# Earlier norm statistics in a Conformer and latent-attention trunk on one core, and a residual loaded row by row

## The chip, the cores and the metric

One core of a Trainium2 chip runs the whole kernel. The metric is the device time of one launch in microseconds (us). The engines are TensorE (PE, matrix products), VectorE (DVE), ScalarE (ACT), GpSimd (POOL) and SyncE (SP, which here issues the DMAs). They run side by side, each in the order of its own program, and wait for one another by semaphores.

## The reference, cut to what matters

The program is two layers on a sequence of 512 rows of 1024 channels in float32. The change touches only the first, the convolution branch:

```
proj = h @ w_in + b_in                      # 1024 -> 3 * 2048
val, glu_gate, z = split(proj, 3)
u = val * sigmoid(glu_gate)
u = causal depthwise convolution of u, 31 taps, + conv_b
u = silu(layer_norm(u, norm_g, norm_b))     # over the 2048 channels
u = u * silu(z)
y = u @ w_out + b_out                       # 2048 -> 1024
h = layer_norm(alpha * h + y, ln_g[0], ln_b[0])
```

The second layer (a shared latent key and value, 16 attention heads, a gate, an output projection, a norm) reads this h. Products are made to float32 accuracy from split operands: each factor is cut into a rounded high part and a low rest, and three matrix products (low by high, high by low, high by high) are summed.

## The kernel before, in words

**Layout.** The 2048 channels of the branch are 16 tiles of 128 partitions by 512 rows of sequence (CT = 16). The input projection makes 48 such tiles ("chunks"): for each tile first value and gate, then 16 chunks for z. A chunk is 24 matmuls (8 slices of the contraction, 3 products each; `columns`, L1445, with the matmuls in L1421). Then the output projection takes its weights in 16 chunks too, 24 matmuls each: chunks 0 to 7 for the left half of the 1024 outputs, 8 to 15 for the right half; chunk n multiplies the branch tiles 2(n mod 8) and 2(n mod 8) + 1 by four blocks of rows. They are called output chunks here, and the z chunks are numbered 0 to 15.

**Weights.** SP loads a chunk into one of two raw buffers. ACT writes its high part (L719) into one of four slots, POOL the low part (L561); PE then waits for both. A raw buffer is free once POOL has taken the low part, so that a load (L402, L437) follows POOL; a slot is free once PE has used it, so that ACT's high part of chunk c waits for PE to finish chunk c - 4. ACT empties PE's bank of z chunk i through silu into `z_a` (`keep_z`, L808), and PE takes four banks in turn for the z chunks.

**The norm over channels.** DVE makes 12 of the 16 convolutions, tap after tap, and adds all tiles into `csum` (L1090). PE multiplies that by a matrix of ones (L1493, "mean") ahead of z chunk 11 (MEAN_AT). DVE then subtracts the mean from each of the 16 tiles (L1158, `centered`), ACT squares each (L819, L823) into four buffers, DVE sums the even squares (L1164, between its subtractions) and POOL the odd ones (L616). Ahead of z chunk 14 (VAR_AT) PE sums both over the channels with matmuls one column wide (L1500, "variance"); it waits there for both sums. DVE adds the epsilon (L1183), POOL raises to -1/2 (L638), ACT makes four diagonal blocks (L865), and ahead of z chunk 15 (SPREAD_AT) PE spreads the factor over all partitions (L1486, "spread"). SQUARES says behind which z chunk ACT squares which tiles and POOL adds the odd ones: tiles 0 to 3 with chunk 14's weights, 4 to 8 with chunk 15's, 9 to 15 with the first output chunk's.

**The branch.** With the spread factor there, each tile t goes through DVE (times the factor, L1188), ACT (silu, L829), DVE (times `z_a`, L1195), ACT (high part, L835) and DVE (low part, L1199), in three rotating banks. ACT's program runs 17 steps of this loop in one piece, with the rest of its work put in by hand at t = 3 (keep z chunk 15) and t = 9 (the high part of output chunk 3). Only behind the loop does it split the weights of output chunk 4 and later. PE's output chunk n needs the tiles it multiplies.

**The residual.** After the last z chunk, SP loads the input rows again (`res`, 2 MB, L445) and three broadcast rows of the norm and of the bias (L446 to L448), all on one semaphore. Only behind them come the loads of output chunks 4 to 15. ACT scales the four rows of `res` by alpha (L883) behind its splits 5 to 8, POOL adds the bias to them (L656) behind its splits 6 to 9. DVE waits for all four rows before it adds the first product to them (L1220).

Of the kernel before, what the change touches and what calls it, by code (L numbers as in the profile page):

```python
# [32 lines left out]
P = 128  # L33
BANK = 512
DEPTH = 2
D_MODEL = 1024
# [19 lines left out]
CT = CONV_WIDTH // P  # L56
RT = SEQ // P
# [12 lines left out]
Z0 = 2 * CT  # L70
OUT0 = Z0 + CT
# [6 lines left out]
SLOTS = 4  # L78
# [34 lines left out]
def trunk_kernel(nc, x, positions, ln_g, ln_b, a_w_in, a_b_in, a_conv_w, a_conv_b, a_norm_g,  # L113
# [3 lines left out]
    x_rows = x.rearrange("b (r p) d -> p (b r) d", p=P)  # L117
# [10 lines left out]
    with ExitStack() as ctx:  # L128
        def sem(name):
            return ctx.enter_context(nc.semaphore(name))  # L130
# [10 lines left out]
        def at(name, base, offset_words, shape, dtype=F32):  # L141
            return nc.alloc_sbuf_tensor_at(name, shape, dtype, offset=base + 4 * offset_words)
# [75 lines left out]
        res = at("res", reg_xt, 0, [P, RT, D_MODEL])  # L218
        ln_rows = at("ln_rows", reg_xt, 8 * TILE, [P, 3, D_MODEL])
# [52 lines left out]
        def piece(parts, lo, hi):  # L272
# [39 lines left out]
            sem("var_ready"), sem("rstd_cols_ready"), sem("rstd_diag_ready"), sem("rstd_spread"), sem("stat_step"))  # L312
        scaled, silu_done, gated, g_hi_ready, g_lo_ready = (
            sem("scaled"), sem("silu_done"), sem("gated"), sem("g_hi_ready"), sem("g_lo_ready"))
        res_landed, res_scaled, res_ready = sem("res_landed"), sem("res_scaled"), sem("res_ready")
        y_done, y_step, var_row_ready, rstd_row_ready, rstd_step, row_ready = (
            sem("y_done"), sem("y_step"), sem("var_row_ready"), sem("rstd_row_ready"),
            sem("rstd_step"), sem("row_ready"))
# [30 lines left out]
        def added_before(n):  # L349

            return sum(1 for _, k in shared_taps[:n] if k > 0)

        SHARES_BEGIN = SHARED_TILES[0] + 2
        MEAN_AT, VAR_AT, SPREAD_AT = 11, 14, 15
        SQUARES = {14: range(0, 4), 15: range(4, 9), OUT0 - Z0: range(9, CT)}
        GATE_BANK = (4, 5, 6)
        RSTD_BANK = 7
        VSUM_BANK = 6
# [36 lines left out]
        def _(sp):  # L395
            def raw_free(c):

                wait(sp, w_hi_ready, c - RAW_SLOTS + 1)
                wait(sp, w_lo_ready, c - RAW_SLOTS + 1)
# [33 lines left out]
            def load_output(c0, n, source):  # L433

                raw_free(c0 + n)
                half, k = n // PASS, 2 * (n % PASS)
                sp.dma_start(w_raw[(c0 + n) % 2][:].rearrange("p (k m) -> p k m", k=2),  # L437
                             source[k:k + 2, :, half * BANK:(half + 1) * BANK].rearrange("k p m -> p k m")
                             ).then_inc(w_landed[(c0 + n) % 2], 16)
# [2 lines left out]
                load_output(OUT0, n, w_out_a)  # L442

            sp.wait_ge(w_used, OUT0)
            sp.dma_start(res[:], x_rows).then_inc(res_landed, 16)  # L445
            sp.dma_start(ln_rows[:, 0, :], ln_g[0:1, :].broadcast_to([P, D_MODEL])).then_inc(res_landed, 16)  # L446
            sp.dma_start(ln_rows[:, 1, :], ln_b[0:1, :].broadcast_to([P, D_MODEL])).then_inc(res_landed, 16)
            sp.dma_start(ln_rows[:, 2, :], a_b_out.broadcast_to([P, D_MODEL])).then_inc(res_landed, 16)  # L448
            for n in range(SLOTS, CT):
                load_output(OUT0, n, w_out_a)  # L450
            for n in range(LATENTS):
                c = LAT0 + n
                raw_free(c)
                if n < KV:
                    load_columns(c % 2, w_down, n * P)
                elif n == KV:
                    halves = w_raw[c % 2][:].rearrange("p (k b m) -> p b k m", b=2, m=ROPE)
                    for b in range(2):
                        sp.dma_start(halves[:, b], w_down[:, :, KV_RANK:KV_RANK + ROPE]
                                     ).then_inc(w_landed[c % 2], 16)  # L460
                else:
                    load_columns(c % 2, w_in_b, (n - KV - 1) * P)
# [80 lines left out]
        def _(pool):  # L543
# [74 lines left out]
            def add_odd_squares(tiles):  # L618
                for t in tiles:
                    if t % 2 == 1 and t > 1:  # L620
                        add_odd_square(t)

            for i in range(CT):
# [7 lines left out]
                for n in z_taps(i):  # L631
                    add_product(n)
                add_odd_squares(SQUARES.get(i, ()))
            split_lo(OUT0, OUT0 % 2, OUT0 % SLOTS)
            add_odd_squares(SQUARES[CT])

            pool.wait_ge(var_ready, 1)
            nc.gpsimd.tensor_tensor(rstd_cols[:], var_cols[:], minus_half[:], ALU.pow).then_inc(rstd_cols_ready, 1)  # L638
# [10 lines left out]
            for k in range(CT):  # L649
                c = OUT0 + k  # L650
                if k > 0:
                    split_lo(c, c % 2, c % SLOTS)
                if 6 <= k < 6 + RT:
                    r = k - 6
                    pool.wait_ge(res_scaled, r + 1)
                    nc.gpsimd.tensor_tensor(res[:, r, :], res[:, r, :], ln_rows[:, 2, :], ALU.add  # L656
                                            ).then_inc(res_ready, 1)
# [57 lines left out]
        def _(act):  # L715
# [54 lines left out]
            def keep_conv(m):  # L770
                t = MATRIX_TILES[m]
                act.wait_ge(*((diag_used, len(TAP_GROUPS)), (pe_conv_done, 1))[m])
                nc.scalar.activation(acc[:, t, :], bank[MATRIX_BANK[m]][:], ACT.Identity,
                                     bias=vec[:, V_CONVB + t:V_CONVB + t + 1]).then_inc(pe_conv_kept, 1)


            for q in range(2 * RT):
                r, half = q // 2, q % 2
# [26 lines left out]
            def keep_z(i):  # L805

                act.wait_ge(w_used, Z0 + i + 1)
                nc.scalar.activation(z_a[:, i, :], bank[i % 4][:], ACT.Silu,  # L808
                                     bias=vec[:, V_BIN + 2 * CT + i:V_BIN + 2 * CT + i + 1]
                                     ).then_inc(evacuated, 1)  # L810
# [5 lines left out]
            def square(t):  # L816
                act.wait_ge(centered, t + 1)
                if t < 2:
                    nc.scalar.activation((bank[VSUM_BANK], vsum_odd)[t][:], acc[:, t, :], ACT.Square  # L819
                                         ).then_inc((vsum_done, vsum_odd_done)[t], 1)  # L820
                else:
                    wait(act, (vsum_done, vsum_odd_done)[t % 2], t // 2 - 1)
                    nc.scalar.activation(sq[t % 4][:], acc[:, t, :], ACT.Square  # L823
                                         ).then_inc((squared_even, squared_odd)[t % 2], 1)
# [12 lines left out]
            def output_split(k):  # L837
                c = OUT0 + k
                split_hi(c, c % 2, c % SLOTS, landed_value(c))

            for i in range(CT):
                z_split(i)
                if i == 0:
                    keep_value_gate(CT - 1, (CT - 1) % ROUND)
                    for g in range(len(TAP_GROUPS)):
                        conv_matrices(1, g)
                        for n in matrix_taps(g):
                            tap_times_u(n)
                    keep_conv(0)
                if i == 2:  # L850
                    keep_conv(1)
                for t in SQUARES.get(i, ()):
                    square(t)
                if i >= 3:
                    keep_z(i - 3)
                for n in z_taps(i):
                    tap_times_u(n)
            output_split(0)
            for t in SQUARES[CT]:
                square(t)  # L860
            keep_z(CT - 3)
            output_split(1)
            act.wait_ge(rstd_cols_ready, 1)
            for b in range(RT):
                nc.scalar.activation(rstd_diag[:, b * P:(b + 1) * P], ident[:], ACT.Copy,  # L865
                                     scale=rstd_cols[:, b:b + 1]).then_inc(rstd_diag_ready, 1)
            keep_z(CT - 2)
            output_split(2)
            for t in range(CT + 1):
                if t == 3:  # L870
                    keep_z(CT - 1)
                if t == 9:
                    output_split(3)
                if t < CT:
                    branch_silu(t)
                if t >= 1:
                    branch_hi(t - 1)
            for k in range(SLOTS, CT):
                output_split(k)
                if 5 <= k < 5 + RT:  # L880
                    r = k - 5
                    act.wait_ge(res_landed, 64)
                    nc.scalar.activation(res[:, r, :], res[:, r, :], ACT.Copy, scale=ALPHA  # L883
                                         ).then_inc(res_scaled, 1)

# [2 lines left out]
            for q in range(2 * RT):  # L888
                r, half = q // 2, q % 2
# [149 lines left out]
        def _(dve):  # L1039
            for q in range(2 * RT):  # L1040
                r, half = q // 2, q % 2
# [205 lines left out]
                                                   ).then_inc(row_ready, 1)  # L1247

            dve.wait_ge(res_ready, RT)
            def turned_lo(r):  # L1250
                for q in (2 * r, 2 * r + 1):
                    cut = (slice(None), slice(4 * (q % 2), 4 * (q % 2) + 4), slice(r * P, (r + 1) * P))
                    dve.wait_ge(ht_hi_ready, q + 1)
                    nc.vector.tensor_tensor(ht_lo[cut], bank[q][:].rearrange("p (k n) -> p k n", k=4),  # L1254
                                            ht_hi[cut].bitcast(F32), ALU.subtract).then_inc(ht_lo_ready, 1)
# [504 lines left out]
```

## Time and profile before

| what | value |
|---|---|
| median of 3 timed runs | 899.72 us (899.52 to 900.37) |
| the profiled execution's own time | 898.75 us |
| its span | 897.0 us |
| PE busy | 860.2 us, 96% of the span |
| DVE busy | 607.1 us, 68% |
| POOL busy | 486.4 us, 54% |
| ACT busy | 399.5 us, 45% |
| mean granted clock of PE | 0.982 |

The table is the first part of the profile's page. The span runs from the first to the last instruction of one profiled execution, and 1.75 us of the execution's own time lie outside it. Times of rows below count from the start of the span. The granted clock is TensorE's: 1.00 is 2.4 GHz and 0.50 is 1.2 GHz.

### The profile page before, as it was taken

What the parts mean: (1) busy time and instruction counts of PE and PEld (TensorE: products, weight loads), DVE (VectorE), ACT (ScalarE), POOL (GpSimd) and SP (SyncE); (2) the same over time, 40 slices, a digit from 0 to 9 for tenths busy, and PEclk for the clock granted to TensorE, in tenths of its full rate; (3) what the DMA queues carried; (4) which work ended last, traced back from release to release, by engine and by line L of the source; (5) the groups of instructions that cost most, each with busy time, mean ns of one, the idle gap of its engine ahead of it and who ended that gap; (6) DMA issues with size and microseconds to landing.
All of it is one profiled execution on the core that took longest, in us unless ns stands there. A gap on an engine that the chain in (4) does not pass through costs nothing.

```text
span 897.0 us, 11802 instructions
## 1 busy us (share of the span) xinstructions
PE 860.2 (96%) x4059; PEld 714.5 (80%) x4059; DVE 607.1 (68%) x1077; ACT 399.5 (45%) x694; POOL 486.4 (54%) x272
## 2 busy tenths in 40 slices
PE   5999999999999989799899999999999999989996
PEld 4888888888888767588698788878988888978885
DVE  2899999999999538420842292039778779768207
ACT  3655444436653447621332344146555565545110
POOL 3578888877995462384654437424324424126443
PEclk7999999999999979899999999999999999999999
DMA  6242333320044325243043334321232320223212
GB/s 205 77 119 76 104 96 95 95 75 0 1 118 118 94 71 188 73 134 98 1 139 109 95 93 130 80 68 41 61 82 70 82 80 13 71 94 141 94 48 95
DMA packets 111351, 78.99 MB, mean 88 GB/s; under 512 B 14023, under 2 KB 98093, under 8 KB 111277
## 3 DMA queue, kind: packets, MB, share of 16 engines
q1 hardware_dynamic: 111308, 78.44, 29.1%
q8 instruction: 24, 0.39, 0.2%
q14 instruction: 19, 0.16, 0.1%
HBM read 71.87 MB, written 2.10 MB: 82 GB/s over the span
## 4 chain that ended last, share of the span: by engine, by line
PE 88%; DVE 4%; issue 2%; POOL 2%; ACT 1%; DMA 1%; SPq 0%; POOLq 0%; DVEq 0%; ACTq 0%
PE bank L1421 83%; PE bank L1686 2%; DMA x_in<-in_x_dram 1%; PE bank L1675 1%; PE bank L1676 1%; DVE bank L1195 1%; DVE g_lo L1199 1%; POOL vsum_odd L616 1%; POOL w_lo L561 1%; DVE res L1245 0%; ACT w_hi L719 0%; PE bank L1432 0%; PE bank L1500 0%; DVE pt_lo L1360 0%; DVE fg_lo L1405 0%
## 5 line engine op out<-in xcount | busy, mean ns | idle before, releaser
L561 POOL TENSOR_TENSOR w_lo<-w_raw,w_hi 128x1024 fp32r<-128x1024 f32 x103 | 253.7, 2472 | 205.6 <-ACT w_hi L719 179.8
L1105 DVE SCALAR_TENSOR_TENSOR bank<-u,conv_w,bank 128x512 f32<-128x512 f32 x348 | 233.5, 750 | 0.9
L1421 PE MATMUL bank<-xt_hi,w_lo 128*128 128x512 f32 x384 | 154.6, 403 | 1.4 <-DVE xt_lo L1044 1.4
L719 ACT ACTIVATE w_hi<-w_raw 128x1024 fp32r<-128x1024 f32 x103 | 107.0, 1053 | 104.8 <-PE bank L1421 52.0
L1421 PE MATMUL bank<-xt_lo,w_hi 128*128 128x512 f32 x384 | 153.4, 399 | 0.0
L1421 PE MATMUL bank<-xt_hi,w_hi 128*128 128x512 f32 x384 | 153.1, 399 | 0.0
L1421 PEld LDWEIGHTS bank<-xt_hi,w_lo 128*128 128x128 f32 x384 | 73.7, 192 | 19.4 <-DVE xt_lo L1044 1.8
L1421 PEld LDWEIGHTS bank<-xt_lo,w_hi 128*128 128x128 f32 x384 | 73.5, 191 | 17.5 <-issue 0.5
L1421 PEld LDWEIGHTS bank<-xt_hi,w_hi 128*128 128x128 f32 x384 | 73.5, 191 | 17.4
L588 POOL TENSOR_TENSOR acc<-acc,tap_product 128x512 f32<-128x512 f32 x60 | 77.9, 1298 | 8.5 <-ACT tap_product L753 1.6
L669 POOL TENSOR_TENSOR bundle_lo<-bundle_raw,bundle_hi 128x1024 fp32r<-128x1024 f32 (+1 forms) x16 | 47.1, 2961 | 62.3 <-ACT bundle_hi L917 62.3
L1421 PE MATMUL bank<-ht_hi,w_lo 128*128 128x512 f32 (+2 forms) x200 | 76.5, 383 | 2.5 <-DVE ht_lo L1254 2.5
L1421 PE MATMUL bank<-ht_lo,w_hi 128*128 128x512 f32 (+2 forms) x200 | 75.7, 379 | 0.0
L1421 PE MATMUL bank<-ht_hi,w_hi 128*128 128x512 f32 (+2 forms) x200 | 75.7, 379 | 0.0
L1220 DVE SCALAR_TENSOR_TENSOR res<-res,bank 128x512 f32<-128x512 f32 x16 | 10.9, 681 | 91.7 <-PE bank L1421 65.3
L1421 PE MATMUL bank<-w_hi,g_lo 128*128 128x512 f32 x128 | 51.8, 405 | 6.1 <-issue 6.1
L753 ACT ACTIVATE tap_product<-u,conv_w 128x512 f32<-128x512 f32 x60 | 41.7, 718 | 32.3 <-POOL acc L588 32.0
L982 ACT ACTIVATE prob<-prob,neg_top 128x512 f32<-128x512 f32 (+1 forms) x64 | 35.5, 555 | 43.5 <-DVE neg_top L1319 43.5
L1421 PE MATMUL bank<-w_hi,fg_lo 128*128 128x512 f32 x128 | 50.9, 398 | 1.2 <-DVE fg_lo L1405 1.2
L1421 PE MATMUL bank<-w_hi,g_hi 128*128 128x512 f32 x128 | 51.0, 399 | 0.0
L1421 PE MATMUL bank<-w_lo,g_hi 128*128 128x512 f32 x128 | 51.0, 398 | 0.0
L1421 PE MATMUL bank<-w_hi,fg_hi 128*128 128x512 f32 x128 | 50.6, 395 | 0.0
(198 smaller groups left out, 1815.4 us busy)
## 6 DMA issues: line engine op xcount, KB each, us to landing
w_raw<-in_a_w_in_dram SPq DMA_DIRECT2D x48, 512.0 KB, 3.7
w_raw<-in_b_w_in_dram SPq DMA_DIRECT2D x20, 512.0 KB, 3.6
w_raw<-in_a_w_out_dram SPq DMA_DIRECT2D x16, 512.0 KB, 3.7
w_raw<-in_b_w_out_dram SPq DMA_DIRECT2D x16, 512.0 KB, 3.5
bundle_raw<-in_b_w_uq_dram SPq DMA_DIRECT2D x16, 256.0 KB, 3.8
x_in<-in_x_dram SPq DMA_DIRECT2D x4, 512.0 KB, 7.0
res<-in_x_dram SPq DMA_DIRECT2D x1, 2048.0 KB, 7.8
bundle_raw<-in_kv_w_uk_dram SPq DMA_DIRECT2D x8, 256.0 KB, 3.0
```

The costliest lines, as they stand in the source:

```text
L561: nc.gpsimd.tensor_tensor(w_lo[slot][:], w_raw[raw][:], w_hi[slot][:].bitcast(F32), ALU.subtract).then_inc(w_lo_ready, 1)
L588: nc.gpsimd.tensor_tensor(acc[:, t, :], acc[:, t, :], tap_product[n % 2][:], ALU.add).then_inc(product_added, 1)
L616: nc.gpsimd.tensor_tensor(vsum_odd[:], vsum_odd[:], sq[t % 4][:], ALU.add).then_inc(vsum_odd_done, 1)
L669: nc.gpsimd.tensor_tensor(bundle_lo[slot][part][:], bundle_raw[:, lo:hi], bundle_hi[slot][part][:].bitcast(F32), ALU.subtract).then_inc(bu ...
L719: nc.scalar.activation(w_hi[slot][:], w_raw[raw][:], ACT.Copy).then_inc(w_hi_ready, 1)
L753: nc.scalar.activation(tap_product[n % 2][:], u[:, t, k:k + SEQ], ACT.Copy, scale=tap).then_inc(product_ready, 1)
L982: nc.scalar.activation(block_, block_, ACT.Exp, bias=neg_top[:, b:b + 1], scale=SM_SCALE, accum_out=denom[:, b:b + 1]).then_inc(exp_done, 1)
L1105: nc.vector.scalar_tensor_tensor(out=bank[CONV_BANK[slot]][:] if k < TAPS - 1 else acc[:, t, :], in0=u[:, t, k:k + SEQ], scalar=conv_w[:, ...
L1195: nc.vector.tensor_tensor(inner[:], inner[:], z_a[:, t, :], ALU.mult).then_inc(gated, 1)
L1220: nc.vector.scalar_tensor_tensor(out=rows_half, in0=rows_half, scalar=scale, in1=bank[RT * half + r][:], op0=ALU.mult, op1=ALU.add).then_i ...
L1421: last = nc.tensor.matmul(out_ap, a, b, start=(start and n == 0 and m == 0), stop=(stop and n == len(parts) - 1 and m == 2))
L1686: last = nc.tensor.transpose(bank[to_bank][:, first + k * P:first + (k + 1) * P], prob[:, (prob_at[b] + k) * P:(prob_at[b] + k + 1) * P], ...
```

## The change

Three things are changed together. The mean, variance and spread stand ahead of z chunks 10, 13 and 14 (before: 11, 14, 15). The squares follow: tiles 0 to 7 with chunk 13's weights, 8 to 15 with chunk 14's, none behind the output weights; ACT keeps each z chunk one step later, and the loop over the branch tiles has its inserted work at t = 3, 6 and 9. The residual and the broadcast rows are loaded in seven pieces, each behind the load of one output chunk, with semaphores of their own; ACT and POOL take the rows one step later.

```diff
-        res_landed, res_scaled, res_ready = sem("res_landed"), sem("res_scaled"), sem("res_ready")
+        res_landed = [sem(f"res_landed{r}") for r in range(RT)]
+        bias_landed, ln_a_landed = sem("bias_landed"), sem("ln_a_landed")
+        res_scaled, res_ready = sem("res_scaled"), sem("res_ready")
...
-        MEAN_AT, VAR_AT, SPREAD_AT = 11, 14, 15
-        SQUARES = {14: range(0, 4), 15: range(4, 9), OUT0 - Z0: range(9, CT)}
+        MEAN_AT, VAR_AT, SPREAD_AT = 10, 13, 14
+        SQUARES = {13: range(0, 8), 14: range(8, CT)}
...
             sp.wait_ge(w_used, OUT0)
-            sp.dma_start(res[:], x_rows).then_inc(res_landed, 16)
-            sp.dma_start(ln_rows[:, 0, :], ln_g[0:1, :].broadcast_to([P, D_MODEL])).then_inc(res_landed, 16)
-            sp.dma_start(ln_rows[:, 1, :], ln_b[0:1, :].broadcast_to([P, D_MODEL])).then_inc(res_landed, 16)
-            sp.dma_start(ln_rows[:, 2, :], a_b_out.broadcast_to([P, D_MODEL])).then_inc(res_landed, 16)
             for n in range(SLOTS, CT):
                 load_output(OUT0, n, w_out_a)
+                r = n - SLOTS - 1
+                if n == SLOTS:
+                    sp.dma_start(ln_rows[:, 2, :], a_b_out.broadcast_to([P, D_MODEL])).then_inc(bias_landed, 16)
+                elif r < RT:
+                    sp.dma_start(res[:, r, :], x_rows[:, r, :]).then_inc(res_landed[r], 16)
+                elif r == RT:
+                    sp.dma_start(ln_rows[:, 0, :], ln_g[0:1, :].broadcast_to([P, D_MODEL])).then_inc(ln_a_landed, 16)
+                elif r == RT + 1:
+                    sp.dma_start(ln_rows[:, 1, :], ln_b[0:1, :].broadcast_to([P, D_MODEL])).then_inc(ln_a_landed, 16)
...
             split_lo(OUT0, OUT0 % 2, OUT0 % SLOTS)
-            add_odd_squares(SQUARES[CT])
...
-                if 6 <= k < 6 + RT:
-                    r = k - 6
+                if 7 <= k < 7 + RT:
+                    r = k - 7
+                    if r == 0:
+                        pool.wait_ge(bias_landed, 16)
                     pool.wait_ge(res_scaled, r + 1)
...
+                if i >= 4:
+                    keep_z(i - 4)
                 for t in SQUARES.get(i, ()):
                     square(t)
-                if i >= 3:
-                    keep_z(i - 3)
...
             output_split(0)
-            for t in SQUARES[CT]:
-                square(t)
-            keep_z(CT - 3)
-            output_split(1)
+            keep_z(CT - 4)
             act.wait_ge(rstd_cols_ready, 1)
...
-            keep_z(CT - 2)
-            output_split(2)
+            output_split(1)
+            keep_z(CT - 3)
             for t in range(CT + 1):
                 if t == 3:
+                    output_split(2)
+                    keep_z(CT - 2)
+                if t == 6:
                     keep_z(CT - 1)
...
-                if 5 <= k < 5 + RT:
-                    r = k - 5
-                    act.wait_ge(res_landed, 64)
+                if 6 <= k < 6 + RT:
+                    r = k - 6
+                    act.wait_ge(res_landed[r], 16)
...
             dve.wait_ge(res_ready, RT)
+            dve.wait_ge(ln_a_landed, 32)
```

## Rows read from the trace of the kernel before

**Rows 1.** The page: busy time by engine; the chain that ended last, by engine.
```profile
PE 860.2 (96%) x4059; PEld 714.5 (80%) x4059; DVE 607.1 (68%) x1077; ACT 399.5 (45%) x694; POOL 486.4 (54%) x272
...
PE 88%; DVE 4%; issue 2%; POOL 2%; ACT 1%; DMA 1%; SPq 0%; POOLq 0%; DVEq 0%; ACTq 0%
```
**Rows 2.** Windows: stretch, its length, busy by engine, granted clock, DMA share, GB/s.
```profile
322.00:325.30 3.30, 0.00 (x0) 0.03 (x1) 0.69 (x1) 2.32 (x4) 2.87 (x3) 0.90 0.22 86
325.30:328.85 3.55, 3.54 (x17) 3.55 (x17) 0.00 (x0) 0.00 (x0) 0.00 (x0) 0.50 0.02 5
```
**Rows 3.** Timeline of PE: start, length, line, count, idle time before and its releaser.
```profile
303.30 1.02 PE L1493 MATMUL bank<-csum,ones 128*128 128x512 f32 x2
...
325.31 0.56 PE L1500 MATMUL bank<-ones,vsum 128*128 128x1 f32 x2 [4.19 <-POOL vsum_odd L616]
...
372.34 0.76 PE L1421 MATMUL bank<-w_hi,g_lo 128*128 128x512 f32 x1 [6.12 <-issue]
...
375.88 0.40 PE L1421 MATMUL bank<-w_hi,g_hi 128*128 128x512 f32 x1
...
447.59 0.66 PE L1421 MATMUL bank<-ht_hi,w_lo 128*128 128x384 f32 x1 [2.45 <-DVE ht_lo L1254]
```
**Rows 4.** The chain that ended last: start, length, what, with counts.
```profile
328.85 8.51 PE bank L1421 x24
337.36 0.86 PE bank L1486 x2
338.22 5.61 PE bank L1421 x24
...
632.61 1.09 PE bank L1686 x10
```
**Rows 5.** Timeline of DVE: the last sum, the subtractions, the branch's start and its pause.
```profile
296.75 0.69 DVE L1090 TENSOR_TENSOR csum<-bank,acc 128x512 f32<-128x512 f32 x1
304.35 3.08 DVE L1158 SCALAR_TENSOR_TENSOR acc<-bank,acc 128x512 f32<-128x512 f32 x5 [6.91 <-PE bank L1493]
...
338.26 1.29 DVE L1188 TENSOR_TENSOR bank<-acc,bank 128x512 f32<-128x512 f32 x2 [9.21 <-PE bank L1486]
...
345.22 0.70 DVE L1195 TENSOR_TENSOR bank<-bank,z_a 128x512 f32<-128x512 f32 x1 [0.31 <-ACT bank L829]
```
**Rows 6.** Timeline of ACT: an ordinary step, squares, diagonal blocks, tile 3, the loop's end.
```profile
297.92 0.69 ACT L808 ACTIVATE z_a<-bank,vec 128x512 f32<-128x512 f32 x1 [3.95 <-PE bank L1421]
298.51 1.05 ACT L719 ACTIVATE w_hi<-w_raw 128x1024 fp32r<-128x1024 f32 x1
...
317.08 2.18 ACT L823 ACTIVATE sq<-acc 128x512 f32<-128x512 f32 x4
...
330.20 1.28 ACT L865 ACTIVATE rstd_diag<-ident,rstd_cols 128x128 f32<-128x128 f32 x4 [5.62 <-POOL rstd_cols L638]
...
344.44 0.74 ACT L829 ACTIVATE bank<-bank,vec 128x512 f32<-128x512 f32 x1
...
368.77 1.99 ACT L719 ACTIVATE w_hi<-w_raw 128x1024 fp32r<-128x1024 f32 x2
```
**Rows 7.** Timeline of POOL: the odd squares, the power, two low parts.
```profile
319.63 5.53 POOL L616 TENSOR_TENSOR vsum_odd<-vsum_odd,sq 128x512 f32<-128x512 f32 x4
329.13 1.04 POOL L638 TENSOR_TENSOR rstd_cols<-var_cols,minus_half 128x4 f32<-128x4 f32 x1 [3.97 <-DVE var_cols L1183]
330.14 2.38 POOL L561 TENSOR_TENSOR w_lo<-w_raw,w_hi 128x1024 fp32r<-128x1024 f32 x1
```
**Rows 8.** Windows behind and around other gaps of PE, columns as in rows 2.
```profile
448.00:449.00 1.00, 1.00 (x4) 1.00 (x4) 1.00 (x2) 0.00 (x0) 0.92 (x2) 0.50 0.24 57
...
590.00:594.00 4.00, 2.49 (x11) 1.76 (x10) 0.69 (x1) 3.23 (x4) 1.57 (x1) 1.00 0.00 0
```
**Rows 9.** DMA issues from 300 to 430 us: count, KB each, us to landing.
```profile
w_raw<-in_a_w_out_dram SPq DMA_DIRECT2D x16, 512.0 KB, 3.7
res<-in_x_dram SPq DMA_DIRECT2D x1, 2048.0 KB, 7.8
```

## The prediction

> **What bounds the kernel now.** I read the page first. PE is busy for 96% of the span and makes 88% of the chain that ended last [rows 1], so only time in which PE stands still, or runs at half clock, can be won. Next the windows by granted clock around the norm: the clock is at 0.50 (1.2 GHz) over the whole variance step [rows 2]. Third, the timeline of PE. It stands still twice near the change: 4.19 us ahead of the variance matmuls, released by POOL's last odd square, and 6.12 us ahead of output chunk 4 [rows 3]. That second gap bears the name "issue", but the chain and ACT's timeline show who it is: ACT's high part of chunk 4 starts only at 368.77, at the end of the branch loop [rows 6]. Fourth, the lengths of chunks in the chain: z chunk 14 takes 8.51 us and z chunk 15 takes 5.61 [rows 4]. Last, the timelines of DVE, ACT and POOL, for the lengths of their steps.
>
> What these stalls cost, as a ceiling: 4.19 + 6.12 us of standing still; 8.51 - 5.61 = 2.9 us of half clock in chunk 14; the variance step, 3.54 us of chain between 325.31 and 328.85 [rows 2, 3]; and the first eight matmuls of output chunk 4, 375.88 - 372.34 = 3.54 us where eight take 5.58 x 8/24 = 1.86, so 1.7 us.
>
> **The unit steps.** A full-clock chunk is 5.58 us of PE: 5.61 in the chain with its tail [rows 4], and I take 5.58 since the last matmul of z chunk 9 releases ACT at 297.92 [rows 6] and the mean starts behind z chunk 10 at 303.30 [rows 3]; so z chunk 10 starts at 303.30 - 5.58 = 297.72. Mean and spread take 0.86 us of PE each (two matmuls) [rows 4]. DVE: five subtractions in 3.08 us [rows 5], so one per (3.08 - 0.69)/4 = 0.60. ACT: four squares in 2.18 [rows 6], 0.52 each, or DVE's pace where it waits for it. POOL: four odd squares in 5.53 [rows 7], about 1.4 each. A low part 2.4 [rows 7], a high part 1.0 [rows 6], the power 1.04 [rows 7], the four diagonal blocks 1.28 [rows 6].
>
> The variance step at full clock is not in this trace. Bounds: its 16 matmuls are load-bound and took 3.54 at half clock; ten transposes with loads of the same size took 1.09 us at full clock [rows 4], so 16 would take 1.74. I take 1.8, nearest to that row and half of 3.54, and keep 3.54 as the other end.
>
> **Mean at chunk 10.** It wants `csum`. DVE writes it at 296.75 + 0.69 = 297.44 [rows 5]; PE arrives at 297.72. So the mean fits with 0.3 us to spare, and what it costs is its place only. Nothing ahead of it moves on DVE. ACT's `keep_z` a step later costs nothing: ACT waited 3.95 us in such a step [rows 6], and PE needs that bank only four chunks on.
>
> **The sums.** Subtractions start 1.05 us behind the mean's start (304.35 - 303.30 [rows 3, 5]), at 298.8. DVE has 16 subtractions and 7 even sums, 23 x 0.60 = 13.8 us. Before, this run was cut in pieces: ACT came back to squares only behind weights and `keep_z`, which wait for PE. Now ACT does high part 13 (297.9 to 298.9), keeps z 9, and squares tiles 0 to 7 at DVE's pace, until 305.5. Then high part 14, z 10 (307.1), tiles 8 to 15; DVE loses 0.6 us there (its even sum 10 waits for square 8) and subtracts tile 15 by 312.6; ACT's square 15 is done at 313.3. POOL does low part 13, odd tiles 3, 5, 7 (306.9), low part 14 (309.3), then tiles 9, 11, 13 and 15 chained: 309.3 + 5.5 = 314.8. PE reaches the variance at 297.72 + 0.86 + 3 x 5.58 = 315.3. So the 4.19 us of standing still go, with 0.5 us to spare, and with them the cause of the half clock; the variance ends at 315.3 + 1.8 = 317.1.
>
> **The spread at chunk 14.** It wants the diagonal blocks at 317.1 + 5.58 = 322.7. Queued on POOL ahead of the power now: low part 15 (314.8 to 317.1) and the first output low part, whose high part ACT can make only when PE is through with z chunk 12 at 315.3 (316.4 done). So POOL: 317.1 to 319.5, power to 320.6; ACT's blocks to 321.9. 0.8 us to spare. Before, the blocks were there at 330.20 + 1.28 = 331.5 for a spread at 337.3 [rows 4, 6], some 6 us of room; most of that is used up.
>
> **The branch.** Spread starts at 322.7, so DVE scales tile 0 at 323.7 (before: 338.26 [rows 5]), 14.5 us earlier. ACT is ready: it makes output chunk 1's high part at 322.8 and keeps z 13, until 324.4, when tile 0 is scaled. One new wait stands in ACT's loop: at t = 3 it makes chunk 2's high part and keeps z 14, and both want z chunk 14, which ends at 322.7 + 0.86 + 5.58 = 329.1. Silu of tile 3 then starts at 329.2 + 1.0 + 0.6 = 330.8, or 7.0 us behind the first scale, where before it started 344.44 - 338.26 = 6.2 behind it [rows 5, 6] and stopped DVE for 0.31. Behind it silus 4 and on queue; DVE's next product comes 0.8 us late, and the whole loop with it. At t = 6 z 15 is kept at about 334.9 to 335.6; z chunk 15 ends at 334.7 and PE writes that bank again at 336.8: hidden. Output chunk 4 followed the first scale by 372.34 - 338.26 = 34.1 us [rows 3, 5]; now 34.1 + 0.8, so it starts at 358.6.
>
> **PE itself** gets to output chunk 4 at 329.1 + 5 x 5.58 = 357.0 (z 15, output 0 to 3; their tiles of the branch come at one per 1.92 us, twice per chunk, and are ready). So 1.6 us of standing still remain, set by the branch loop. I assume that this gap leaves the clock alone.
>
> **The residual.** Before: 2 MB and three rows of 0.5 MB in one piece ahead of output load 4. Now each piece follows a load that must wait for POOL's low parts: bias behind load 4 at 334.7; row 0 behind load 5 at about 344; row 1 behind load 6 at about 359; rows 2 and 3 one chunk apart. A load of 0.5 MB took 3.7 us and the 2 MB 7.8 [rows 9], and a chunk takes 5.58, so each row is there when ACT's split of the same step is: row r is issued ahead of weight load r + 6, and ACT asks for it behind split r + 6. POOL adds 2.4 us to its 2.4 for four steps, 4.8 of 5.58. The fourth row is ready a chunk later, near the end of output chunk 7, and DVE's half rows (about 5.5 us) lie beside chunk 8; the first row norm comes with chunk 12. I cost all this at nothing; without that cover a late row costs one for one.
>
> The Trainium skill speaks against the cut: "DMA: Bandwidth & Descriptors", section Bandwidth, asks for transfers of 1 MiB or more for at least 75% of peak. By that rule four rows take longer than one block, and the trace agrees: 4 x 3.7 = 14.8 us against 7.8 [rows 9]. It would change the time only in the slower rival below.
>
> **The sum.** Output chunk 4 starts 372.34 - 358.6 = 13.7 us earlier and runs at full clock (1.7): 15.4 us. Beside the ceiling: 4.2 + 2.9 + 1.7 (variance) + 6.1 + 1.7 = 16.6, less 1.6 left; the two agree within 0.4. All behind output chunk 4 moves along, since PE bounds it. From the execution profiled, 898.75 becomes 883.4; that execution is 1.0 us below the median of 899.72. On the median: 884.4.
>
> **Rivals.**
> *The clock still falls at the variance.* For: one-column matmuls and transposes are little work; behind some transposes and 2.45 us of standing still the clock was at 0.50 [rows 3, 8]. Against: a stretch with only 2.49 of 4.00 us of matmuls kept 1.00 [rows 8], and here 1.8 us of variance lie between full chunks. Cost: the variance at up to 3.54 instead of 1.8, and up to 2.9 us in chunk 13, 1.7 to 4.6 in all: near 887.
> The Trainium skill, "TensorE: Matmul & The Clock Gate", section on what is happening in Part 1, says that the throttled state is the default and activity releases it. By that rule the variance step is at risk although PE is never idle; the time would be this rival's.
> *A link is late.* The margins are 0.3, 0.5 and 0.8 us, out of chains of up to 17 us; 3% more on POOL's or ACT's chain and PE waits at variance or spread. It costs the lateness, 1 to 3 us, and with a fallen clock more: 886 to 889.
> *The clock falls in the gap ahead of output chunk 4*, 1.6 us of it: 1.7 us more, 886.1.
> *The gain is hidden* (within 0.2%): the mean would have to wait for `csum` by some 14 us. DVE's rows speak against it [rows 5].
> *Slower: the rows of the residual starve PE.* POOL and ACT take them in order, and a row that lands late holds back the next low part. It decides once a row and a weight load together take more than a chunk with 2 us of slack, 7.6 us; two loads at 3.7 are 7.4 if they do not overlap at all. With four rows landing late by up to 3.7 us and 1.7 us of clock each, 4 x 5.4 = 21.6 - 15.4 = 6.2 us slower, 905.9. Against it: loads before overlapped (the 2 MB in 7.8).
>
> **How the numbers follow.** Forecast 55%; fallen clock at the variance 17%; late link 14%; clock at chunk 4 6%; hidden 3%; slower 3%; 2% for more gain than the sum (no gap, cheaper variance: 882.7). The range, 882.8 to 889.2, holds all but some 15%. What a measurement of this kernel can tell from no change is about 0.2%, 1.8 us. Faster by more than that: 0.94; within it 0.03; slower 0.03.
>
> **What would show it.** Right: mean at 297.7 and variance at 315.3 with no idle time ahead of them; granted clock 1.00 and a chunk 13 of 5.6 us; spread at 322.7; a pause of DVE of some 1.1 us at the branch's tile 3; output chunk 4 at 358.6 behind 1.6 us of idle PE. Wrong: a window at 0.50 behind the variance (the clock rival); PE released by POOL's L616 or ACT's L865 (a late link); ACT's L719 or L883 waiting for DMA between chunks 5 and 11 with PE idle (the slower rival).

## The result, and the profile after

| | median us | runs | span of the profiled execution |
|---|---|---|---|
| before | 899.62 | 4 | 897.0 |
| changed | 886.88 | 3 | 884.3 |

The changed kernel took 886.41, 886.88 and 888.78 us; a fourth execution, 1065.4 us at a mean granted clock of 0.749, is left out, and with it the median of all four is 887.83. The ratio to the kernel before is 0.986 (95% interval 0.9836 to 0.9883): faster by 1.4%. The forecast was 884.4 in a range of 882.8 to 889.2. Run again on another chip, with experiments 6 to 8, the changed kernel took 885.68 us against 900.12 (ratio 0.9842, 0.9829 to 0.9856).

The page of the changed kernel, busy time and the chain by engine, as [rows 1]: PE is busy for 2.5 us less in a span 12.7 us shorter, so most of what went was time in which PE stood still. Its share of the chain is 92% instead of 88.

```profile
PE 857.7 (97%) x4059; PEld 712.7 (81%) x4059; DVE 606.3 (69%) x1077; ACT 399.4 (45%) x694; POOL 487.1 (55%) x272
...
PE 92%; DVE 2%; DMA 2%; SPq 1%; issue 1%; ACT 1%; POOL 0%; POOLq 0%; DVEq 0%; ACTq 0%
```

The chain that ended last, from z chunk 8 to the output projection (start, length, what):

```profile
289.85 9.30 PE bank L1430 x40
299.14 0.86 PE bank L1502 x2
300.00 16.73 PE bank L1430 x72
316.73 1.68 PE bank L1509 x16
318.41 5.68 PE bank L1430 x24
324.09 0.86 PE bank L1495 x2
324.94 33.59 PE bank L1430 x144
358.53 1.55 issue
360.09 61.83 PE bank L1430 x264
```

Before, pieces of POOL, ACT and DVE stood between PE's. Two of them, POOL's sum of odd squares ahead of the variance and DVE's low part in the branch loop:

```profile
319.68 1.25 POOL vsum_odd L616
...
345.92 0.60 DVE g_lo L1199
```

Now it is PE from end to end: mean, three chunks (16.73 = 3 x 5.58), variance in 1.68 us, chunk 13 in 5.68 (before, chunk 14 behind the variance took 8.51 [rows 4]), spread, six chunks, one gap of 1.55, and on. The clock, in windows with the columns of [rows 2], stays at full speed through the variance and through the gap:

```profile
316.00:318.00 2.00, 2.00 (x18) 1.86 (x16) 0.00 (x0) 1.17 (x2) 2.00 (x2) 1.00 0.04 8
318.00:320.00 2.00, 2.00 (x12) 1.69 (x12) 0.16 (x1) 0.46 (x1) 2.00 (x2) 1.00 0.07 17
...
358.00:360.00 2.00, 0.53 (x3) 0.09 (x1) 0.00 (x0) 0.49 (x1) 2.00 (x2) 1.00 0.00 0
360.00:362.00 2.00, 1.91 (x8) 1.61 (x9) 0.00 (x0) 0.00 (x0) 2.00 (x1) 1.00 0.31 92
```

The three engines that feed PE, by their timelines: DVE's last sum, its subtractions, its first product of the branch and its pause at tile 3 (as [rows 5]); ACT's last square, the diagonal blocks, silu of tile 3 and the end of its loop (as [rows 6]); POOL's last odd squares, the two low parts ahead of the power, and the power (as [rows 7]).

```profile
296.46 0.69 DVE L1098 TENSOR_TENSOR csum<-bank,acc 128x512 f32<-128x512 f32 x1
300.04 3.08 DVE L1166 SCALAR_TENSOR_TENSOR acc<-bank,acc 128x512 f32<-128x512 f32 x5 [2.89 <-PE bank L1502]
...
324.98 1.29 DVE L1196 TENSOR_TENSOR bank<-acc,bank 128x512 f32<-128x512 f32 x2 [6.37 <-PE bank L1495]
...
332.94 0.70 DVE L1203 TENSOR_TENSOR bank<-bank,z_a 128x512 f32<-128x512 f32 x1 [1.31 <-ACT bank L837]
```
```profile
313.76 0.63 ACT L831 ACTIVATE sq<-acc 128x512 f32<-128x512 f32 x1 [0.56 <-DVE acc L1166]
...
321.80 1.28 ACT L870 ACTIVATE rstd_diag<-ident,rstd_cols 128x128 f32<-128x128 f32 x4 [3.34 <-POOL rstd_cols L644]
...
330.64 1.06 ACT L727 ACTIVATE w_hi<-w_raw 128x1024 fp32r<-128x1024 f32 x1 [1.54 <-PE bank L1430]
...
332.17 0.74 ACT L837 ACTIVATE bank<-bank,vec 128x512 f32<-128x512 f32 x1
...
356.50 2.00 ACT L727 ACTIVATE w_hi<-w_raw 128x1024 fp32r<-128x1024 f32 x2
```
```profile
310.48 5.62 POOL L623 TENSOR_TENSOR vsum_odd<-vsum_odd,sq 128x512 f32<-128x512 f32 x4
316.06 4.71 POOL L568 TENSOR_TENSOR w_lo<-w_raw,w_hi 128x1024 fp32r<-128x1024 f32 x2
320.73 1.04 POOL L644 TENSOR_TENSOR rstd_cols<-var_cols,minus_half 128x4 f32<-128x4 f32 x1
```

Compare their ends with PE's starts, which are those of its timeline: odd squares ready at 310.48 + 5.62 = 316.1, variance at 316.57; blocks ready at 321.80 + 1.28 = 323.1, spread at 323.93. Both fit, by 0.5 and 0.8 us.

### The profile page after: what moved, and what is told of

It is laid out like the page before. It is cut to its first block, busy times and chain, and to the rows that moved or that the text cites. A ratio compares the mean times of both kernels' runs of the same rounds, so it can differ in the third digit from the quotient of the medians.

```text
span 884.3 us, 11806 instructions
## 1 busy us (share of the span) xinstructions
PE 857.7 (97%) x4059; PEld 712.7 (81%) x4059; DVE 606.3 (69%) x1077; ACT 399.4 (45%) x694; POOL 487.1 (55%) x272
## 4 chain that ended last, share of the span: by engine, by line
PE 92%; DVE 2%; DMA 2%; SPq 1%; issue 1%; ACT 1%; POOL 0%; POOLq 0%; DVEq 0%; ACTq 0%
PE bank L1430 88%; PE bank L1695 1%; DMA pos_int<-in_positions_dram 1%; PE bank L1684 1%; PE bank L1685 1%; SPq L421 1%; DVE pt_lo L1369 0%; DVE res L1253 0%; DVE prob L1339 0%; DMA qr_stack<-qr_lo 0%; SPq L414 0%; ACT prob L990 0%; PE bank L1568 0%; PE bank L1622 0%; PE bank L1509 0%
## 5 line engine op out<-in xcount | busy, mean ns | idle before, releaser
L699 POOL TENSOR_TENSOR qr_raw<-qr_raw,cos 128x512 f32<-128x512 f32 x8 | 10.4, 1294 | 72.6 <-DMA qr_swap<-qr_raw 72.6
```

The costliest lines, as they stand in the source:

```text
L699: nc.gpsimd.tensor_tensor(qr_raw[:], qr_raw[:], cos[:], ALU.mult).then_inc(rope_step, 1)
```

## The experiments

The start of the span takes longer in one profile than in another, by up to 3.6 us. PE begins z chunk 10, or the mean that stands ahead of it, at 297.7 us before the change, at 299.0 in the changed kernel and at up to 301.3 in the experiments. The difference is there by 36 us of the span, and the clock has a part in it. PE between 24 and 30 us, before and changed, with the columns of [rows 2]:

```profile
24.00:30.00 6.00, 6.00 (x39) 4.81 (x38) 5.42 (x7) 4.22 (x6) 2.37 (x2) 1.00 0.04 11
```
```profile
24.00:30.00 6.00, 5.79 (x30) 4.80 (x31) 5.60 (x7) 4.52 (x6) 2.67 (x2) 0.72 0.04 11
```

The granted clock is 1.00 here and 0.72 there, and 0.50 in experiment 1. From 36 to 290 us PE is busy at 1.00 in all these profiles.

Beside each time I therefore give the **stretch**: from the start of z chunk 10, or of the mean ahead of it, to the end of the span. Before it is 897.0 - (303.30 - 5.58) = 599.3 us; changed, 884.3 - 298.98 = 585.3. Experiments 1 to 4 ran on one chip, 5 to 8 on a second and 9 on a third, each beside runs of the kernel before (900.47, 900.12 and 900.44 us). Across chips the ratios to these are compared.

**1. The norm's steps alone.** The residual stays as before.

Its edit against the kernel before, without ACT's and POOL's order, which is that of the change:

```diff
-        MEAN_AT, VAR_AT, SPREAD_AT = 11, 14, 15
-        SQUARES = {14: range(0, 4), 15: range(4, 9), OUT0 - Z0: range(9, CT)}
+        MEAN_AT, VAR_AT, SPREAD_AT = 10, 13, 14
+        SQUARES = {13: range(0, 8), 14: range(8, CT)}
...
```

> Only the first part of the change: mean, variance and spread ahead of z chunks 10, 13 and 14, with the squares and ACT's order as in the changed kernel; the residual and the broadcast rows are loaded in one piece ahead of output load 4 and taken by ACT and POOL at the steps of the kernel before. Theory (all of the gain is PE's standing still and half clock around the norm, and the residual's cut is neutral): 887 us, within 1 us of the changed kernel; PE idle 0 at the variance, output chunk 4 at about 360 us of the span. Rival (the cut of the residual gives part of the gain, because 3.5 MB ahead of output load 4 delay weights): 889 to 891, with ACT waiting for the DMA of output chunk 4 or 5 and a PE gap of over 3 us ahead of chunk 4.

885.43 us, against 900.47 before (ratio 0.9834, 0.982 to 0.9847); stretch 884.9 - 300.43 = 584.5; the gap ahead of output chunk 4 is 1.56. That is 1.6 us under the 887 expected. The first theory holds: this part has the whole gain.

**2. The residual alone.**

Its edit against the changed kernel, again without ACT's and POOL's order, which is that of the kernel before:

```diff
-        MEAN_AT, VAR_AT, SPREAD_AT = 10, 13, 14
-        SQUARES = {13: range(0, 8), 14: range(8, CT)}
+        MEAN_AT, VAR_AT, SPREAD_AT = 11, 14, 15
+        SQUARES = {14: range(0, 4), 15: range(4, 9), OUT0 - Z0: range(9, CT)}
...
```

> Only the second part: the residual in four rows and the broadcast rows, each behind one output load, ACT and POOL one step later; the norm's steps stand as in the kernel before. Theory (neutral): 899.7 us, within 1 us of the kernel before; DVE's first half row a chunk's third later, hidden. Rival (four small transfers collide with weight loads, as the changed kernel's trace hints, where ACT waited 5.75 us for output chunk 6's weights against 4.31 before): 901 to 903, with idle PE ahead of output chunks 6 to 9.

900.46 against 900.47 (ratio 0.9999, 0.999 to 1.0009); stretch 899.6 - (305.93 - 5.58) = 599.3, as before. Neutral. The gap ahead of output chunk 4 is the old one, 6.12.

**3. The squares cut as before**, on the changed kernel.

```diff
-        SQUARES = {13: range(0, 8), 14: range(8, CT)}
+        SQUARES = {13: range(0, 4), 14: range(4, 9), 15: range(9, CT)}
```

> The changed kernel with the squares cut as in the kernel before: tiles 0 to 3 with chunk 13's weights, 4 to 8 with chunk 14's, 9 to 15 with chunk 15's. Theory (PE stood still at the variance because ACT and POOL came back to squares only behind steps that wait for PE): PE reaches the variance at 316.6, POOL makes low part 15 first (from 312.1) and ends the odd squares at 320.1, so 3.6 us idle; 890.5 if the clock holds, up to 895 if it falls for the variance and part of chunk 13. Rival (the order of the squares is indifferent and only the mean's place mattered): 887, no idle time ahead of the variance.

893.9 us (ratio 0.9925, 0.991 to 0.994), stretch 891.8 - 300.35 = 591.5: 6 to 8 us more than the changed kernel's two profiles (585.3, and 583.5 in experiment 5). Its chain, with POOL back in it, and the clock:

```profile
313.74 2.42 POOL w_lo L568
316.16 1.27 POOL vsum_odd L623
...
321.80 3.55 PE bank L1509 x16
325.35 7.13 PE bank L1430 x24
```
```profile
318.00:321.80 3.80, 0.09 (x1) 0.03 (x1) 1.09 (x2) 2.82 (x5) 3.51 (x4) 0.97 0.32 115
321.80:325.30 3.50, 3.50 (x17) 3.50 (x17) 0.00 (x0) 0.00 (x0) 2.16 (x1) 0.50 0.04 12
```

PE stands still for 3.71 us, where 3.6 was expected. The fallen clock adds 3.55 - 1.68 = 1.87 at the variance and 7.13 - 5.68 = 1.45 in the chunk behind it: 7.0 us, as the stretch of experiment 1 has it too (591.5 - 584.5). The wait cost nearly twice its length.

**4. Output chunk 4's high part inside the branch loop**, on the changed kernel.

```diff
                 if t == 9:
                     output_split(3)
+                if t == 13:
+                    output_split(SLOTS)
...
             for k in range(SLOTS, CT):
-                output_split(k)
+                if k > SLOTS:
+                    output_split(k)
```

> The changed kernel with the high part of output chunk 4 made inside ACT's branch loop, at t = 13, instead of behind it. Theory (the 1.55 us gap of PE ahead of output chunk 4 is only ACT's program order): the gap goes, output chunk 4 starts at about 358.5 us of the span, 1.5 us less than the changed kernel, 885.4. Rival (the branch tiles or the following chunks then become late, as DVE's loop loses the high part's 1 us): gap moves to chunk 5 or 6, 887.

884.5 us (ratio 0.982, 0.9806 to 0.9834), with PE not idle at chunks 4, 5 and 6; stretch 883.8 - 300.91 = 582.9. The median is 0.9 us below experiment 1 on the same chip, but the intervals of the two ratios overlap, so the medians alone do not show a gain. The traces do, up to the start of the second layer: the gap is gone and PE gets there 1.8 us sooner (the table below). Behind that the first latent matmuls met a fallen clock for longer (7.24 us for 24, 5.97 in experiment 1), which hides part of it.

**5. The changed kernel again**, without an edit.

> The changed kernel itself once more, so that the other kernels of this call are compared on one chip. If the 1 to 3 us by which its first four timed runs differ are the start of the launch and the clock's timing (the small loads of the start land at 24 to 26 us of the span, whatever the kernel), its median lies between 885 and 888 and its stretch from the mean to the end at 584 to 586 us, as the first profile's 585.3. If the piecewise residual costs something, it stays over 1 us above the kernel with the norm's steps alone (885.43).

885.68 us (885.01 to 887.33); stretch 883.0 - 299.47 = 583.5. The median is in the expected range and the stretch 0.5 us below it. The ratio, 0.9842, is that of experiment 1 (0.9834) within their intervals: the residual's cut costs nothing that these runs can tell.

**6. Variance and spread one chunk later.**

```diff
-        MEAN_AT, VAR_AT, SPREAD_AT = 10, 13, 14
+        MEAN_AT, VAR_AT, SPREAD_AT = 10, 14, 15
```

> The changed kernel with variance and spread one z chunk later (ahead of 14 and 15, as before the change), mean and squares as changed. Theory (output chunk 4 follows the spread by a fixed 36 us of the branch's loop, so each chunk that the spread comes later is paid at output chunk 4): no idle time at the variance, PE idle 1.55 + 5.6 - 0.8 = 6.3 us ahead of output chunk 4, and the clock falls there for eight matmuls (1.7): 6.3 us more than the changed kernel, 893. Rival (the gain came from the variance's wait alone): 887, gap at chunk 4 unchanged.

889.62 us (ratio 0.9889, 0.987 to 0.9907), stretch 887.3 - 299.58 = 587.7: 4.2 us more than in experiment 5 where 6.3 were expected. The theory had the direction right and the place wrong. PE's timeline has two gaps:

```profile
341.65 0.50 PE L1430 MATMUL bank<-w_hi,g_lo 128*128 128x512 f32 x1 [2.85 <-ACT z_a L816]
...
364.85 0.47 PE L1430 MATMUL bank<-w_hi,g_lo 128*128 128x512 f32 x1 [1.09 <-issue]
```

The first is one that I had not seen coming: ACT keeps z chunk 15 at the loop's t = 6, which now comes too late for output chunk 0, whose fourth block of rows wants that bank. Behind it the clock is down for a while:

```profile
342.00:344.00 2.00, 2.00 (x7) 1.62 (x6) 1.97 (x4) 1.35 (x3) 0.00 (x0) 0.62 0.60 244
344.00:346.00 2.00, 2.00 (x6) 1.51 (x6) 1.97 (x5) 1.34 (x3) 0.00 (x0) 0.52 0.00 0
```

Gaps of 2.85 + 1.09 against 1.56 make 2.4 us, and 87 matmuls to chunk 4 in 22.11 us where 87 x 5.58/24 = 20.2 make 1.9 more: 4.3. Output chunk 4 still follows the spread, by 364.85 - 330.10 = 34.8 us here and 360.57 - 324.41 = 36.2 in experiment 5.

**7. The variance three times over**, the same result each time.

```diff
-                    for b in range(RT):
+                    for b in [b for _ in range(3) for b in range(RT)]:
```

> The changed kernel with the variance's 16 one-column matmuls done three times over (48, the same result each time), at 1.68 us for 16. Theory (the clock fell before the change because PE stood still, and one-column matmuls do not lower it): 5.0 us of variance at a granted clock of 1.00, everything behind it 3.4 us later, 890.3. Rival (so little work in the array lowers the clock by itself, given time): granted clock 0.50 within the variance, its rest at twice the time and up to 2.9 us more in z chunk 13: 893 to 896.

893.97 us, stretch 893.5 - 300.59 = 592.9: 9.4 us more than experiment 5. The rival was right. PE never stands still, and the clock falls all the same, within the one-column matmuls:

```profile
318.34 7.21 PE bank L1509 x48
325.55 8.48 PE bank L1430 x24
```
```profile
320.00:321.00 1.00, 1.00 (x12) 1.00 (x11) 0.00 (x0) 0.07 (x1) 1.00 (x2) 1.00 0.00 0
321.00:322.00 1.00, 1.00 (x8) 1.00 (x8) 0.00 (x0) 0.00 (x0) 1.00 (x1) 0.65 0.52 174
322.00:323.00 1.00, 1.00 (x6) 1.00 (x7) 0.00 (x0) 0.00 (x0) 0.33 (x1) 0.50 0.79 305
```

3.4 us for 32 more matmuls at full clock, 7.21 - 5.0 = 2.2 for half clock on them, 8.48 - 5.68 = 2.8 in chunk 13: 8.4 of the 9.4, and the remaining 1.0 lies behind the first layer (the table below). The other runs took 892.97, 894.97 and 888.81 us. The last is even below the 890.3 of the first theory, and its mean granted clock is 0.992 where the profiled execution has 0.982: the clock fell for less time in it, if at all. So this fall is not certain in every execution.

**8. The norm's steps, the residual in one piece, and experiment 4's edit.**

> The norm's steps of the changed kernel, the residual in one piece as in the kernel before, and the high part of output chunk 4 inside ACT's branch loop at t = 13. Theory (the gap ahead of output chunk 4 is worth 1.5 us, the residual's cut nothing): as the earlier kernel with this edit, 884.5, and 1.5 us below the norm's steps alone. Rival (the 3.5 MB in one piece now collide with output chunk 4, which is wanted 1.5 us sooner): 886.

884.18 us (ratio 0.9816, 0.9802 to 0.9829), the lowest median of all, though not told apart from experiment 4 (0.982); stretch 883.2 - 301.28 = 581.9. It is 1.5 us less than experiment 5 by the medians of one chip, with ranges that touch (883.2 to 885.05 against 885.01 to 887.33). To the start of the second layer its trace takes as long as experiment 4's, with the residual in one piece here and in seven there.

**9. The mean ahead of chunk 9.**

```diff
-        MEAN_AT, VAR_AT, SPREAD_AT = 10, 13, 14
+        MEAN_AT, VAR_AT, SPREAD_AT = 9, 13, 14
```

> The changed kernel with the mean one z chunk earlier still, ahead of chunk 9; variance, spread and squares as changed. Theory (the mean's place at chunk 10 is the earliest at which DVE's last sum is there, and a place too early is paid by PE one for one): PE reaches the mean at about 293.5 us of the span where the last sum is ready near 297.2, so 3.5 to 5 us idle ahead of the mean, perhaps with a fallen clock behind it (up to 2.5), and nothing given back since output chunk 4 still follows the spread: 889 to 893. Rival (the earlier start of the subtractions gives back at variance and branch what PE loses at the mean): 885.7, as the changed kernel.

889.17 us (ratio 0.9877, 0.9851 to 0.9902; the changed kernel has 0.9842, 0.9829 to 0.9856, so the intervals just overlap; 3.5 us by the medians). PE waits for DVE's last sum, 2.70 us where 3.5 to 5 were expected, and the clock holds:

```profile
296.71 1.10 PE L1502 MATMUL bank<-csum,ones 128*128 128x512 f32 x2 [2.70 <-DVE csum L1098]
```
```profile
294.00:297.00 3.00, 0.30 (x2) 0.30 (x2) 2.46 (x4) 1.63 (x2) 1.76 (x1) 1.00 0.46 138
297.00:300.00 3.00, 3.00 (x13) 2.11 (x12) 2.16 (x4) 0.00 (x0) 0.59 (x1) 1.00 0.30 83
```

Nothing gives the wait back: from the start of z chunk 10 itself, behind the mean, to the second layer PE takes 425.34 - (297.81 + 5.58) = 121.95 us here and 422.40 - 300.49 = 121.91 in experiment 5.

**All profiles in three parts.** PE's first transposes for the second layer mark the end of the first. Before and changed, from the chains:

```profile
435.79 0.45 PE bank L1559 x4
```
```profile
421.91 0.45 PE bank L1568 x4
```

This gives three parts of each span, in us: up to z chunk 10 or the mean ahead of it, from there to these transposes, and the rest.

| kernel | up to z chunk 10 | to the second layer | behind |
|---|---|---|---|
| before | 297.72 | 138.07 | 461.2 |
| changed | 298.98 | 122.93 | 462.4 |
| changed again (experiment 5) | 299.47 | 122.93 | 460.6 |
| norm's steps alone (1) | 300.43 | 122.95 | 461.5 |
| residual alone (2) | 300.35 | 137.77 | 461.5 |
| late squares (3) | 300.35 | 129.97 | 461.5 |
| with chunk 4's high part in the loop (4) | 300.91 | 121.15 | 461.7 |
| the same, residual in one piece (8) | 301.28 | 121.15 | 460.8 |
| late variance (6) | 299.58 | 127.11 | 460.6 |
| variance three times (7) | 300.59 | 131.27 | 461.6 |

The middle part is the same to 0.02 us in the three profiles with the norm's steps of the change. The others differ by 3.6 and 1.8 us without following the change.

## Why the prediction was right, step by step

**What bounds the kernel: right.** PE's idle time and half clock near the norm could be won, and they were: before, 4.19 and 6.12 us of idle time [rows 3], now 0 and 1.55.

**Mean at chunk 10: right.** It fits (296.46 + 0.69 = 297.15 against a mean at 298.98), and experiment 9 shows that chunk 9 is too early. The margin is 1.8 us where 0.3 was forecast, mostly because PE came 1.3 us later in this execution. Whether 0.3 would have been enough was not put to the test: no profile of the changed kernel has a start as early as the one before.

**The sums: right, term by term.** Forecast 0.5 us to spare at the variance, measured 316.57 - 316.10 = 0.5. The variance at full clock was taken as 1.8 us and is 1.68. Experiment 3 shows that the place of the squares alone brings the wait back, with the mean at chunk 10.

**The spread: right.** Forecast 0.8 to spare, measured 0.8.

**The branch: right.** Forecast: ACT held up at t = 3, and output chunk 4 34.9 us behind the first scale with 1.6 us of gap. Measured: ACT idle for 1.54 and DVE for 1.31 there, 360.09 - 324.98 = 35.1, a gap of 1.55 with the clock at 1.00. Experiments 4 and 8 show that the gap is ACT's program order: with the high part inside the loop it is gone, and PE reaches the second layer 1.8 us sooner.

**The residual at nothing: right in time.** Experiments 1, 2 and 5 show it on both sides of the other part. The cover is thinner than I had it: ACT waited 5.75 us for output chunk 6's weights, and the 0.5 MB rows took a median 5.4 us to land where I used the 3.7 of a weight load [rows 9]. That agrees with what the Trainium skill says against small transfers ("DMA: Bandwidth & Descriptors", section Bandwidth): 4 x 5.4 us against 7.8 for the block. But each row was issued right behind a weight load, and how much of the 5.4 is the load beside it no run separates. Chunk 6 was still in time. From the list of DMA issues between 300 and 430 us:

```profile
w_raw<-in_a_w_out_dram SPq DMA_DIRECT2D x16, 512.0 KB, 3.9
res<-in_x_dram SPq DMA_DIRECT2D x4, 512.0 KB, 5.4
```

**The sum: right for the first layer, with two terms missing outside it.** Forecast 15.4 us off the profiled execution; it lost 898.75 - 886.41 = 12.3. The part that the forecast worked out, from z chunk 10 to the second layer, went from 138.07 to 122.93: 15.1 us of the 15.4. The forecast took all else as unchanged, and that was the step at fault for the other 3 us:

- The kernel before was profiled in an execution with an early start, 297.72 against 298.98: 1.3 us.
- Behind the first layer the changed profile has 462.4 us against 461.2: 1.2 us. Of these, 0.9 are the latents' first 24 matmuls, which took 6.87 us instead of 5.95 at a fallen clock (the chains of the two kernels):

```profile
433.72 6.87 PE bank L1430 x24
```
```profile
447.59 5.95 PE bank L1421 x24
```

- Outside the span lie 886.41 - 884.3 = 2.1 us against 1.75: 0.4 us.

Together 15.1 - 1.3 - 1.2 - 0.4 makes 12.3 before rounding. None of the three follows the change: experiment 1, with the same norm's steps, took 5.97 us for those 24 matmuls, and experiment 5, the same kernel, is 1.8 us shorter behind the first layer. The forecast of 884.4 missed the median of 886.88 by 2.5 us, and that of 885.68 on another chip by 1.3; both are of the size of such variation. By medians the gain was 12.7 us on the first chip and 14.4 on the second.

**The rivals.** The clock's fall at the variance did not come, but experiment 7 shows that its ground was sound: 16 one-column matmuls kept 1.00, 48 did not. Nor did the clock fall in the gap ahead of output chunk 4. A late link did not come either; experiments 3, 6 and 9 show what one costs, some 7, 4 and 3.5 us. The slower rival (starving weights) did not show in experiment 2; in the changed kernel ACT waited for weights by DMA up to 5.75 us at a time between chunks 6 and 12, but PE was never idle there.

## What to carry to other kernels

Where an engine that bounds the kernel waits for a chain over three others, write each one's program out in order with start and end times: steps that wait for the bounding engine itself, placed ahead of the chain's steps in another queue, are what stretches it. A wait of PE can cost more than its length: those of 3.71 and 2.85 us cost 3.3 and 1.9 us more here, because the clock fell behind them, and one of 2.70 only 0.1. And compare profiles between common events rather than from the span's start: here the start varied by up to 3.6 us and the end by 1.8, and the part between two events inside agreed to 0.02.

## What was not expected of the hardware

A PE that was busy without a break lost its clock: in the profile of experiment 7, 48 matmuls one column wide, with their loads, ran at 1.00 for the first 3.0 us and at 0.50 from about 321.3, and the chunk behind them ran 14 matmuls before it was back. The Trainium skill ("TensorE: Matmul & The Clock Gate", Part 1) has the throttled state as the default that activity releases. In this trace PE was busy in every window and the clock fell all the same, so being busy did not by itself keep it.

Nor does the length of a gap settle it. Gaps of 1.55 us (changed) and 2.70 (experiment 9) left the clock at 1.00. Gaps of 2.85 (experiment 6), 3.71 (experiment 3), 4.19 and 6.12 [rows 3] were followed by 0.50. And the same wait of PE, ahead of the first latents, went both ways: 2.45 us with 0.50 behind it in the kernel before [rows 3, 8] and in the changed one, and 2.46 us with 1.00 throughout in experiment 5, where these 24 matmuls took 4.4 us. What made the difference no run here shows.
